# Norm sums inside the next projection's first tile, a third PSUM unit for the p-tiles, and tables made in the preceding feed-forward

## The chip, the core and the metric

The kernel is one program on one core of a Trainium2 chip. TensorE (PE in the rows) does matrix products into PSUM, VectorE (DVE) and ScalarE (ACT) do elementwise work, GpSimd (POOL) does elementwise work too, SyncE (SP) issues transfers. Each engine runs its own queue in order and waits on semaphores. The metric is the device time of one execution in microseconds, lower is better.

## What is computed

A two-layer decoder trunk for 512 prompt tokens and 8 x 8 sample tokens, so T = 576 columns, model width 1024 (8 blocks of 128 rows).

```python
def rms_norm(x, g, eps=1e-6):
    y = xf * lax.rsqrt(jnp.mean(xf * xf, axis=-1, keepdims=True) + eps)
    return (y * g.astype(jnp.float32)).astype(x.dtype)

def trunk(x, p, even_states, odd_past, W):
    for l in range(DEPTH):
        h = h + 0.5 * swiglu(rms_norm(h, W['ffn_norm1'][l]), W['ffn1_wi'][l], W['ffn1_wo'][l])
        hn = rms_norm(h, W['mix_norm'][l])
        ...
        h = h + mix
        h = h + 0.5 * swiglu(rms_norm(h, W['ffn_norm2'][l]), W['ffn2_wi'][l], W['ffn2_wo'][l])
        gate = jax.nn.sigmoid(rms_norm(h, W['ple_norm'][l]) @ W['ple_wg'][l])
        h = h + gate * (p[l] @ W['ple_wp'][l])
    return rms_norm(h, W['final_norm']), new_even, new_odd
```

The mixer of layer 0 is a 31-tap convolution beside an mLSTM, that of layer 1 is differential attention beside stick-breaking attention. There are nine norms, numbered m = 0 to 8 here as in the code: 0 and 4 before a first feed-forward, 1 and 5 before a mixer, 2 and 6 before a second feed-forward, 3 and 7 before the gated embedding (called ple), 8 at the end.

## The kernel before

Activations lie transposed: `h` is 8 blocks of [128 rows, 576 tokens]. Every product is done in a split form: an operand is rounded to a high part (`wr`, `xr`, `hr`), the rest is its low part (`wl`, `xl`, `hl`), and three matmuls (high x high, high x low, low x high: lines 399 to 401) make one product. The 576 tokens are two halves of 288, so one row block k of an output tile is 6 matmuls, and a tile of eight row blocks is 48.

**Weights** come in blocks of up to 2048 columns, in two buffers (slot 0 and slot 1). For each block SP loads `raw` (line 340), ACT rounds it to `wr` (`round_block`, line 807), POOL makes `wl` (line 389), and the semaphore `w_split0` or `w_split1` lets PE start the block. ACT rounds the block after next only when PE is done with the slot and ACT has come to it in its own queue: in each phase ACT's loop over blocks first rounds, then does the elementwise work of that block's tiles.

**A norm.** The gain is put into `xr` by ACT (`head`, line 836) and `xl` by DVE (`rest`, line 1210), without the factor 1/rms. ACT squares each block of `h` (`square`, line 826), DVE adds the squares into `acc` (lines 1219 and 1276), PE sums `acc` over partitions with a matrix of ones into PSUM banks 4 and 5 (`norm_sum`, line 441), ACT takes the root (`root`, line 841), DVE the reciprocal R (`factor`, line 1233), and R multiplies each output tile of the next projection as DVE reads it from PSUM (`normed`, line 1240). In PE's queue `norm_sum(m)` stands ahead of the projection that uses norm m.

**PSUM.** Output tiles alternate between unit 0 (banks 0, 1) and unit 1 (banks 2, 3). Unit 2 is banks 4 and 5, the norm sums and transposes; banks 6 and 7 hold convolution sums and bias rows in other stages.

**The ple phase** has 8 blocks. Block j has a gate tile (8 row blocks, 48 matmuls) and a p-tile (2 row blocks, 12 matmuls). Per block DVE scales the gate tile into `tg`, ACT takes the sigmoid `sg`, DVE multiplies the p-tile by it (`tu`) and adds to `h`, ACT squares, then ACT rounds the next weights. Ahead of it `praw` (p, transposed) is loaded, `pr` rounded by ACT (line 1055) and `pl` made by DVE (line 1581).

**Between feed-forward 2 and layer 1's attention** (norm 5) ACT issues 20 small transfers of bias tables from a scratch in memory (`strip`, `sstrip`, lines 1068 and 1075), and DVE adds masks to them (lines 1616 to 1621) and makes the scalar lambda (lines 1602 to 1612). For norms 2, 4 and 6 the `head` calls stand after the whole preceding phase, because `xr` is still being read by it.

**The start.** POOL clears both `raw` buffers (line 382) before SP may load them. ACT takes h's eight blocks in turn, and rounds the first weight block after block 4. **The end.** DVE makes R whole, then eight products with the gain, each stored by itself.

Of the kernel before, what the change touches and what calls it, by code (L numbers as in the profile page):

```python
# [16 lines left out]
F32 = mybir.dt.float32  # L17
# [101 lines left out]
def build(nc, A):  # L119
# [50 lines left out]
    brel = sb("brel", [32, HEADS * P], at=z)  # L170
    bone = sb("bone", [32, GL], at=z)
    grep = sb("grep", [P, GL], at=z)
    z = [ZONE]
    praw = sb("praw", [P, KP, T], at=z)
# [159 lines left out]
    def _(e):  # L334
# [8 lines left out]

        def load_cache(job):
# [13 lines left out]
        for name in order:  # L358
            p = ph[name]
            if name != ("out", 1):  # L360
                with e.Fori(0, p.nb // 2) as i:
                    load_pair(p, i)
                continue
# [15 lines left out]
    @block.gpsimd  # L379
    def _(e):  # L380
        for s in range(2):
            e.memset(raw[s][:], 0.0).then_inc(S(f"w_split{s}"), 1)
        for name in order:
            p = ph[name]
            with e.Fori(0, p.nb // 2) as i:
                for s in range(2):

                    e.wait_ge(S("w_rounded"), i * 2 + (p.n0 + s + 1))
                    e.tensor_tensor(wl[s][:, 0:p.width], raw[s][:, 0:p.width],  # L389
                                    wr[s][:, 0:p.width].bitcast(F32), ALU.subtract  # L390
                                    ).then_inc(S(f"w_split{s}"), 1)
# [3 lines left out]
    def _(e):  # L395
# [7 lines left out]
        def gemm(name, rhs, ready, after=None):  # L403


            p = ph[name]
            with nullcontext() if after else e.Fori(0, p.nb // 2) as loop:
                for i in range(p.nb // 2) if after else (loop,):
                    for s in range(2):
                        e.wait_ge(S(f"w_split{s}"), i + (p.n0 // 2 + 2))  # L410
                        off = 0
                        for tile, kn_ in enumerate(p.ks):
                            t = s * p.T + tile
                            u = t % 2

                            e.wait_ge(S("tile_evacuated"), i * (2 * p.T) + (p.t0 + t - 2 + 1 + CR_EVAC))
                            for k in range(kn_):
                                need = ready(tile, k) if s == 0 else None
                                if need:
                                    e.wait_ge(S(need[0]), need[1])  # L420
                                a, b = off + k * P, off + (k + 1) * P
# [1498 lines left out]
```

## Time and profile before

| | us |
|---|---|
| median of 3 runs | 2768.86 |
| lowest and highest | 2763.19, 2770.34 |
| the profiled execution, its own time | 2769.76 |
| its span, first to last instruction | 2768.0 |
| granted TensorE clock, mean | 0.945 |
| PE busy | 2614.2 |

The profile is one execution. A row of the order of time reads: start in us, duration in us, engine, line, operation, output<-input, shape, count, and in brackets the idle time before it and what ended that. Rows of matmuls overlap, as they are pipelined: the pace is the difference of their starts. A table of stretches gives each stretch's length, an engine's busy time and in brackets the number of its instructions that touch the stretch, then PEclk, the share of full clock granted (1.00 is 2.4 GHz, 0.5 is 1.2 GHz).

### The profile page before, as it was taken

How to read it: one execution, taken by the hardware profiler on the slowest of the kernel's cores; microseconds unless marked ns; L12 is line 12 of the kernel's file. 1: busy time of each engine (PE TensorE's matmuls, PEld its weight loads, DVE VectorE, ACT ScalarE, POOL GpSimd, SP SyncE). 2: the span in 40 equal slices, each digit the busy share in tenths (PEclk: the TensorE clock that was granted, in tenths of full speed). 3: DMA queues.
4: the chain of work that ended last, by engine and by line, in shares of the span. 5: the costliest groups of instructions: out<-in, count | busy, mean ns of one | idle time of the engine just before them, and what ended most of it. 6: DMA issues, size and time to landing. Idle time of an engine off the chain costs nothing. (4 is left out here: it accounts for less than half of the span.)

```text
span 2768.0 us, 44745 instructions
## 1 busy us (share of the span) xinstructions
PE 2614.2 (94%) x18322; PEld 2469.6 (89%) x18322; DVE 921.4 (33%) x1558; ACT 826.3 (30%) x998; POOL 811.5 (29%) x206
## 2 busy tenths in 40 slices
PE   6999999997889999999999999999789799999997
PEld 6999999984589999999999999999455599999997
DVE  3211224686733211223421122311755432202234
ACT  4321223223114322233432222311444433312232
POOL 3333333320022333333333333332000033333332
PEclk9999999997789999999999999999876699999999
DMA  3222223411012222222222221334311022222122
GB/s 142 78 77 100 76 69 103 84 62 45 33 63 76 79 77 88 85 66 85 91 76 83 84 90 58 112 111 152 97 61 46 16 70 82 69 98 76 68 85 72
DMA packets 66890, 220.39 MB, mean 80 GB/s; under 512 B 14006, under 2 KB 31286, under 8 KB 51194
## 3 DMA queue, kind: packets, MB, share of 16 engines
q1 hardware_dynamic: 50448, 199.49, 20.7%
q10 hardware_dynamic: 16362, 19.81, 2.5%
q8 instruction: 52, 0.85, 0.1%
q14 instruction: 28, 0.23, 0.0%
HBM read 207.95 MB, written 11.33 MB: 79 GB/s over the span
## 5 line engine op out<-in xcount | busy, mean ns | idle before, releaser
L389 POOL TENSOR_TENSOR wl<-raw,wr 128x2048 fp32r<-128x2048 f32 (+2 forms) x200 | 807.8, 4039 | 1928.7 <-ACT wr L807 1928.7
L399 PE MATMUL ps<-xr,wr 128*128 128x288 f32 x4096 | 1224.5, 299 | 8.2 <-DVE xl L1757 3.2
L400 PE MATMUL ps<-xl,wr 128*128 128x288 f32 x4096 | 1215.0, 297 | 0.0
L401 PE MATMUL ps<-xr,wl 128*128 128x288 f32 x4096 | 1210.6, 296 | 0.0
L399 PEld LDWEIGHTS ps<-xr,wr 128*128 128x128 f32 x4096 | 775.1, 189 | 12.2 <-issue 6.4
L401 PEld LDWEIGHTS ps<-xr,wl 128*128 128x128 f32 x4096 | 777.8, 190 | 0.0
L400 PEld LDWEIGHTS ps<-xl,wr 128*128 128x128 f32 x4096 | 776.1, 189 | 1.2
L807 ACT ACTIVATE wr<-raw 128x2048 fp32r<-128x2048 f32 (+1 forms) x200 | 351.7, 1759 | 373.2 <-PE ps L401 299.5
L400 PE MATMUL ps<-hl,wr 128*128 128x288 f32 x1408 | 415.3, 295 | 0.0
L401 PE MATMUL ps<-hr,wl 128*128 128x288 f32 x1408 | 415.0, 295 | 0.0
L399 PE MATMUL ps<-hr,wr 128*128 128x288 f32 x1408 | 413.2, 293 | 0.0
L399 PEld LDWEIGHTS ps<-hr,wr 128*128 128x128 f32 x1408 | 264.7, 188 | 0.9 <-DVE tu L1240 0.9
L400 PEld LDWEIGHTS ps<-hl,wr 128*128 128x128 f32 x1408 | 264.7, 188 | 0.0
L401 PEld LDWEIGHTS ps<-hr,wl 128*128 128x128 f32 x1408 | 264.5, 188 | 0.0
L1240 DVE TENSOR_TENSOR tu<-ps,R 128x576 f32<-128x576 f32 x96 | 72.8, 758 | 502.2 <-PE ps L401 502.2
L854 ACT ACTIVATE hr<-hd 128x576 f32 x88 | 60.3, 686 | 582.3 <-DVE hd L1256 582.3
L1240 DVE TENSOR_TENSOR tg<-ps,R 128x576 f32<-128x576 f32 x111 | 84.1, 758 | 328.1 <-PE ps L401 327.5
L1269 DVE SCALAR_TENSOR_TENSOR h<-ps,h 128x576 f32 x64 | 48.5, 758 | 413.1 <-PE ps L401 413.1
L851 ACT ACTIVATE sg<-tg 128x576 f32<-128x576 f32 x88 | 60.5, 687 | 205.3 <-DVE tg L1240 205.3
L836 ACT ACTIVATE xr<-h,prm 128x576 fp32r<-128x576 f32 (+1 forms) x64 | 47.3, 770 | 168.8 <-DVE h L1269 167.6
L1260 DVE TENSOR_TENSOR hl<-hd,hr 128x576 f32 x88 | 66.8, 759 | 91.4 <-ACT hr L854 91.4
L1329 DVE SCALAR_TENSOR_TENSOR ps<-up,prm,ps 128x512 f32<-128x512 f32 x116 | 87.5, 755 | 3.4 <-DVE us L1365 0.9
(305 smaller groups left out, 1690.5 us busy)
## 6 DMA issues: line engine op xcount, KB each, us to landing
raw<-in_up SPq DMA_DIRECT2D x88, 1024.0 KB, 4.8
raw<-in_down SPq DMA_DIRECT2D x32, 768.0 KB, 4.3
raw<-in_mixin SPq DMA_DIRECT2D x24, 1024.0 KB, 4.8
raw<-in_down SPq DMA_DIRECT2D x32, 640.0 KB, 3.8
raw<-in_ple SPq DMA_DIRECT2D x16, 640.0 KB, 3.8
raw<-in_mixout SPq DMA_DIRECT2D x8, 1024.0 KB, 4.9
kc<-in_kc SPq DMA_DIRECT2D x32, 256.0 KB, 3.4
vc<-in_vc SPq DMA_DIRECT2D x32, 256.0 KB, 3.4
```

The lines of the kernel that those rows point to most:

```text
L389: e.tensor_tensor(wl[s][:, 0:p.width], raw[s][:, 0:p.width], wr[s][:, 0:p.width].bitcast(F32), ALU.subtract).then_inc(S(f"w_split{s}"), 1)
L399: e.matmul(out, wrt, xrt, start=first, stop=False)
L400: e.matmul(out, wrt, xlt, start=False, stop=False)
L401: return e.matmul(out, wlt, xrt, start=False, stop=last)
L807: e.activation(wr[slot][:, 0:w], raw[slot][:, 0:w], ACT.Copy).then_inc(S("w_rounded"), 1)
L836: e.activation(xj, hj, ACT.Copy, scale=prm[:, bass.ds(j + g0, 1)]).then_inc(S("xr_ready"), 1)
L851: e.activation(sg[:], tg[:], ACT.Silu).then_inc(S("silu_ready"), 1)
L854: e.activation(hr[:, bass.ds(i * 2 + s, 1), :].rearrange("p a t -> p (a t)"), hd[:], ACT.Copy).then_inc(S("hr_ready"), 1)
L1240: ins = e.tensor_tensor(two(out), unit(u), two(R[:]), ALU.mult)
L1260: e.tensor_tensor(q, hd[:], r.bitcast(F32), ALU.subtract).then_inc(S("hidden_ready"), 1)
L1269: e.scalar_tensor_tensor(hj, unit(s), 0.5, hj, ALU.mult, ALU.add).then_inc(S("tile_evacuated"), 1)
L1329: a = e.scalar_tensor_tensor(outp, inp, w, accp, ALU.mult, ALU.add)
```

## The change

- `norm_sum(m)` for m = 0 to 7 is no longer ahead of the projection; it is emitted inside the first tile, after row block k = 6 of 8. The first pair of blocks of each projection is taken out of its loop for that. ACT's `root(m)` moves behind the first `round_block` of the phase.
- A second pair of x buffers (`xr2`, `xl2`) serves norms 2, 4 and 6, so that `head` and `rest` run inside the out and ple phases.
- In the ple phase gate tiles alternate between units 0 and 1, and p-tiles use unit 3 (banks 6, 7).
- `praw` is loaded, and `pl` made, in the preceding feed-forward's part of the queues. The bias tables are loaded by SP behind the last `down` weights, and DVE prepares them ahead of `factor(5)`; lambda follows the second tile of the attention projection. Other small tables move likewise.
- At the start the clearing of `raw` is gone, the first rounding follows h's block 0, and the first two low parts are made by POOL in four pieces each.
- At the end ACT multiplies the gain into `h` block by block in the last ple phase, DVE inverts R in halves, and four products and four stores take the place of eight.

```diff
@@ tensor
+        def unit_of(p, t):
+            return t % 2 if p.src != "ple" else 3 if t % 2 else t // 2 % 2
+        def free_before(p, t, first):
+            return 3 if p.src == "ple" and t % 2 == 0 and (t or not first) else 2
+        def gemm_pair(p, i, rhs, ready=None, after=None, norm=None):
...
+                        if norm is not None and (s, tile, k) == (0, 0, kn_ - 2):
+                            norm_sum(norm)
...
-        norm_sum(2)
         ffn(1, 2)
-        norm_sum(3)
...
@@ scalar
-        def blocks(name):
+        def blocks(name, norm=None):
             p = ph[name]
             for n in range(p.nb):
                 if not (name == order[-1] and n == p.nb - 1):
                     round_block(name, n // 2, n % 2)
+                if n == 0 and norm is not None:
+                    root(norm)
                 yield n
...
         for j in range(KD):
+            if j == 1:
+                round_block(order[0], 0, 0, first=True)
             head(0, j, (S(f"h_loaded{j}"), 16))
             square(0, j, None)
-            if j == KD // 2:
-                round_block(order[0], 0, 0, first=True)
...
         def ple(l):
             m = 4 * l + 4
-            e.dma_start(praw[:], A["pT"][l]).then_inc(S("p_loaded"), 16)
             name = ("ple", l)
-            for n in blocks(name):
-                if n == 0:
-                    e.wait_ge(S("p_loaded"), 16 * (l + 1))
-                    e.activation(pr[:], praw[:], ACT.Copy).then_inc(S("pr_ready"), 1)
+            e.wait_ge(S("p_loaded"), 16 * (l + 1))
+            e.activation(pr[:], praw[:], ACT.Copy).then_inc(S("pr_ready"), 1)
+            for n in blocks(name, 4 * l + 3):
                 e.wait_ge(S("tile_evacuated"), evac_at(name, 2 * n))
                 e.activation(sg[:], tg[:], ACT.Sigmoid).then_inc(S("ple_sig"), 1)
-                square(m, n, (S("ple_added"), KD * l + n + 1))
-            if l == 0:
-                heads_after(m)
-            root(m)
+                if l == 0:
+                    head(m, n, (S("ple_added"), KD * l + n + 1))
+                    square(m, n, None)
+                else:
+                    square(m, n, (S("ple_added"), KD * l + n + 1))
+                    e.activation(h[:, n, :], h[:, n, :], ACT.Copy, scale=W("gains", 8 * KD + n)
+                                 ).then_inc(S("h_gained"), 1)
+            if l:
+                root(m)
@@ gpsimd
         for s in range(2):
-            e.memset(raw[s][:], 0.0).then_inc(S(f"w_split{s}"), 1)
+            e.nop().then_inc(S(f"w_split{s}"), 1)
...
+        low_parts(ph[order[0]], 0, 4)
@@ vector
+            if n % 2:
+                split_p(n // 2)
+            if n == 2:
+                odd_tables()
             factor(m + 1)
...
-        for j in range(KD):
-            g = W("gains", 8 * KD + j)
-            e.scalar_tensor_tensor(h[:, j, :], h[:, j, :], g, R[:], ALU.mult, ALU.mult).then_inc(S("y_ready"), 1)
+        for hf in range(2):
+            rh = R[:, hf * HALF:(hf + 1) * HALF]
+            e.reciprocal(rh, rh).then_inc(S("R_ready"), 1)
+            e.wait_ge(S("R_ready"), 9 + hf)
+            for j in range(0, KD, 4):
+                hh = h[:, j:j + 4, hf * HALF:(hf + 1) * HALF]
+                e.tensor_tensor(hh, hh, rh.unsqueeze(1).broadcast_to([P, 4, HALF]), ALU.mult
+                                ).then_inc(S("y_ready"), 1)
```

How ACT's queue reads from the end of feed-forward 3 into the second ple phase (`wr_54` is slot 0, `wr_56` slot 1). Before:

```order
750 L841 ACTIVATE R<-ps,eps_68 128x576
751 L1050 DMA praw<-in_pT 128x1152
752 L807 ACTIVATE wr_56<-raw_53 128x1280
753 L1055 ACTIVATE pr<-praw 128x1152
754 L1057 ACT_TABLE_LOAD
755 L1057 ACTIVATE sg<-tg 128x576
756 L826 ACTIVATE sq<-h 128x576
757 L807 ACTIVATE wr_54<-raw_52 128x1280
```

And in the changed kernel:

```order
791 L1105 ACTIVATE pr<-praw 128x1152
792 L851 ACTIVATE wr_56<-raw_53 128x1280
793 L887 ACT_TABLE_LOAD
794 L887 ACTIVATE R<-ps,eps_68 128x576
795 L1108 ACT_TABLE_LOAD
796 L1108 ACTIVATE sg<-tg 128x576
797 L872 ACTIVATE sq<-h 128x576
798 L1114 ACTIVATE h<-h,prm 128x576
799 L851 ACTIVATE wr_54<-raw_52 128x1280
```

The root is now behind the rounding of slot 1, and there is one more pass over `h` between the square and the rounding of slot 0 (in the first ple phase it is the `xr` pass, `head`).

How DVE's queue reads from the end of feed-forward 2 into the attention projection. Before:

```order
753 L1276 TENSOR_TENSOR acc<-acc,sq 128x576
754 L1264 REGISTER_ALU
755 L1264 COMPARE_AND_BRANCH
756 L1233 RECIPROCAL R<-R 128x576
757 L1602 TENSOR_TENSOR lamt<-prm 128x128
```

And in the changed kernel:

```order
767 L1322 TENSOR_TENSOR acc<-acc,sq 128x576
768 L1310 REGISTER_ALU
769 L1310 COMPARE_AND_BRANCH
770 L1339 TENSOR_TENSOR strip<-strip,cst 128x128 x4
771 L1341 TENSOR_TENSOR sbias<-cst,sstrip 128x64 x4
772 L1344 MEMSET qbd 128x640
773 L1279 RECIPROCAL R<-R 128x576
```

The eight table sums and the clearing now stand between the last sum of squares and the reciprocal.

## Rows read from the trace of the kernel before

**Rows 1.** The page: busy time of each engine, its share, its instructions.
```profile
PE 2614.2 (94%) x18322; PEld 2469.6 (89%) x18322; DVE 921.4 (33%) x1558; ACT 826.3 (30%) x998; POOL 811.5 (29%) x206
```

**Rows 2.** Stretches of PE: length, busy (instructions), PEclk, DMA share, GB/s.
```profile
900.00:1200.00 300.00, 300.00 (x2257) 1.00 0.23 80
455.30:467.00 11.70, 9.29 (x44) 0.71 0.74 174
837.00:846.00 9.00, 6.64 (x35) 0.81 0.01 3
1263.40:1275.00 11.60, 7.93 (x36) 0.71 0.35 109
1334.90:1344.00 9.10, 5.88 (x30) 0.81 0.31 116
1762.00:1774.00 12.00, 8.32 (x40) 0.72 0.49 158
...
2679.40:2694.00 14.60, 10.93 (x67) 0.88 0.40 130
```

**Rows 3.** Order of time around norm 7 and the ple phase: PE, DVE, ACT, POOL.
```profile
2683.41 2.29 PE L441 MATMUL ps<-acc,ones 128*128 128x288 f32 x4 [3.67 <-DVE acc L1276]
...
2682.60 0.75 DVE L1276 TENSOR_TENSOR acc<-acc,sq 128x576 f32<-128x576 f32 x1
2686.51 3.75 DVE L1233 RECIPROCAL R<-R 128x576 f32<-128x576 f32 x1 [3.16 <-ACT R L841]
...
2692.35 0.54 DVE L1225 MEMSET acc<- 128x576 f32 x1
2692.92 0.76 DVE L1240 TENSOR_TENSOR tg<-ps,R 128x576 f32<-128x576 f32 x1
...
2680.93 0.77 ACT L836 ACTIVATE xr<-h,prm  x1 [5.42 <-DVE h L1269]
...
2689.65 1.17 ACT L1055 ACTIVATE pr<-praw 128x1152 fp32r<-128x1152 f32 x1 [2.01 <-DMA praw<-in_pT]
...
2697.94 2.94 POOL L389 TENSOR_TENSOR wl<-raw,wr 128x1280 fp32r<-128x1280 f32 x1 [7.28 <-ACT wr L807]
```

**Rows 4.** Order of time in the first ple phase: DVE, ACT, POOL.
```profile
1277.85 0.76 DVE L1240 TENSOR_TENSOR tg<-ps,R 128x576 f32<-128x576 f32 x1 [0.98 <-PE ps L401]
...
1281.62 1.90 ACT L807 ACTIVATE wr<-raw 128x2048 fp32r<-128x2048 f32 x1
...
1283.59 2.96 POOL L389 TENSOR_TENSOR wl<-raw,wr 128x1280 fp32r<-128x1280 f32 x1 [8.88 <-ACT wr L807]
```

**Rows 5.** Order of time after norm 5: DVE, POOL, PE.
```profile
1777.55 0.89 DVE L1616 TENSOR_TENSOR strip<-strip,cst 128x128 f32<-128x128 f32 x4
1778.36 0.62 DVE L1618 TENSOR_TENSOR sbias<-cst,sstrip 128x64 f32<-128x64 f32 x4
...
1778.88 4.61 POOL L389 TENSOR_TENSOR wl<-raw,wr 128x2048 fp32r<-128x2048 f32 x1 [15.45 <-ACT wr L807]
...
1783.62 0.40 PE L399 MATMUL ps<-xr,wr 128*128 128x288 f32 x1 [1.01 <-POOL wl L389]
```

**Rows 6.** Order of time at the start: POOL, DVE, PE.
```profile
16.14 4.51 POOL L389 TENSOR_TENSOR wl<-raw,wr 128x2048 fp32r<-128x2048 f32 x1 [11.84 <-ACT wr L807]
...
16.83 4.43 DVE L1210 SCALAR_TENSOR_TENSOR xl<-h,prm,xr 128x576 fp32r<-128x576 f32 x1 [1.55 <-ACT xr L836]
...
26.74 0.85 PE L399 MATMUL ps<-xr,wr 128*128 128x288 f32 x1
...
41.56 0.30 PE L399 MATMUL ps<-xr,wr 128*128 128x288 f32 x1
```

**Rows 7.** Order of time at the end: PE, DVE.
```profile
2753.38 1.24 PE L441 MATMUL ps<-acc,ones 128*128 128x288 f32 x4 [3.22 <-DVE acc L1219]
...
2755.42 3.75 DVE L1233 RECIPROCAL R<-R 128x576 f32<-128x576 f32 x1 [2.10 <-ACT R L841]
2759.21 5.92 DVE L1764 SCALAR_TENSOR_TENSOR h<-h,prm,R 128x576 f32<-128x576 f32 x8
```

More of the change, by code:

```diff
@@ L381, in _, with low_parts @@
         for s in range(2):
-            e.memset(raw[s][:], 0.0).then_inc(S(f"w_split{s}"), 1)
+            e.nop().then_inc(S(f"w_split{s}"), 1)
+        def low_parts(p, i, pieces=1):
+            for s in range(2):
+                e.wait_ge(S("w_rounded"), i * 2 + (p.n0 + s + 1))
+                n = p.width // pieces
+                for q in range(pieces):
+                    c = slice(q * n, (q + 1) * n)
+                    ins = e.tensor_tensor(wl[s][:, c], raw[s][:, c], wr[s][:, c].bitcast(F32), ALU.subtract)
+                ins.then_inc(S(f"w_split{s}"), 1)
+        low_parts(ph[order[0]], 0, 4)
         for name in order:
             p = ph[name]
[L385 to L391, printed above, removed]
+            with e.Fori(1 if name == order[0] else 0, p.nb // 2) as i:
+                low_parts(p, i)
     @block.tensor
@@ new lines, in gemm, with xin @@
+        def gemm(name, rhs, ready=None, after=None, norm=None):
+            p = ph[name]
+            gemm_pair(p, 0, rhs, ready, after, norm)
+            if after:
+                for i in range(1, p.nb // 2):
+                    gemm_pair(p, i, rhs, None, after)
+            elif p.nb > 2:
+                with e.Fori(1, p.nb // 2) as i:
+                    gemm_pair(p, i, rhs)
+        def xin(m):
+            xr_, xl_ = x_slot(m)
+            return lambda tile, k: (xr_[:, k, :], xl_[:, k, :])
@@ L779, in _ @@
         e.wait_ge(S("oc_root"), 2 * HEADS)
-        gemm(("out", 1), xin, lambda tile, k: ("mix_ready", KD + k + 1) if tile == 0 else None)
-        norm_sum(6)
+        gemm(("out", 1), xin(5), lambda tile, k: ("mix_ready", KD + k + 1) if tile == 0 else None)
         ffn(3, 6)
-        norm_sum(7)
         ple(1)
@@ L855, in up_phase @@
                                  ).then_inc(S("hr_ready"), 1)
+            if norm is not None:
+                pair(0)
+            with e.Fori(0 if norm is None else 1, p.nb // 2) as i:
+                pair(i)
         def down_phase(n, c, m_next):
@@ L1085, in _ @@
         for kind in range(2):
-            for n in blocks(f"qk{kind}"):
+            for n in blocks(f"qk{kind}", None if kind else 5):
+                if kind == 0 and n == 0:
+                    e.preload_act_table_set("natural_log_exp_and_others")
+                    e.wait_ge(S("lam_sums"), 1)
+                    e.activation(nlam[:, 0:2], nlam[:, 2:4], ACT.Exp).then_inc(S("lam_exp"), 1)
                 if kind and n < 2:
@@ L1558, in _ @@
         new_states(HEADS - 1)
-        def rests(m):
-            for j in range(KD):
-                rest(m, j)
         def out_and_norm(name, m):
```

249 lines of the change are left out of this document (132 added, 117 removed).

## Prediction

> **What bounds the kernel now.** I read the page first. PE is busy for 2614 of 2768 us, every other engine for a third or less [rows 1], so the time is PE's, and only what makes PE wait or run slowly can give anything back. Then PE's stretches. In an undisturbed one 2257 matmuls touch 300 us [rows 2], a pace of 0.133 us for each, at full clock. A norm is different: PE's last matmul before it starts, the last block of h goes through DVE, ACT and DVE, and only when the sum of squares is complete does the norm sum run (2682.60 plus 0.75, then 2683.41) [rows 3]. PE waited 3.67 us there, the granted clock fell to half, so the four norm matmuls took 2.29 us, and the next ones were slow too.
>
> What each norm costs is the length of a stretch less its matmuls at 0.133 us, two fewer than the row counts, since two only touch its edges [rows 2]. Norm 1: 11.7 - 42 x 0.133 = 6.1 us. Norm 2: 9.0 - 33 x 0.133 = 4.6, and I take norm 6, the same edge after an out phase, as 4.6 too. Norm 3: 7.1. Norm 4: 5.4. Norm 5: 6.9, and 1.0 more where PE waits for the low part of slot 1 at 1783.62, because ACT had issued 20 table transfers ahead of that rounding [rows 5]. Norm 7: 14.6 - 65 x 0.133 = 6.0. Together 41.7 us.
>
> **What the move of the norm sums gives.** With norm_sum behind row block 6, PE has 7 x 6 = 42 matmuls, 5.6 us, to do while the last block of h is made. Counted from the start of the last matmul of the old phase, the last sum of squares is complete after 3.9 us (2682.60 + 0.75, less 2679.4, the start of the norm 7 stretch) [rows 2, 3], so both the sum and the last xl are in time and the wait goes, with the clock's fall. What stays is four matmuls in the stream at full clock. They took 1.24 us at the end of the kernel [rows 7], against 0.53 for four at pace: 0.7 us. Seven times that is 4.9, so 41.7 - 4.9 = 36.8 us are to be had, if nothing else is late. The same reasoning covers norms 2, 4 and 6 only because xr2 lets head and rest run early; their cost of about 0.8 us for each block on ACT and DVE hides under tiles of 6.4 us (48 x 0.133).
>
> **What is late next: R.** It now comes from a sum that starts at 5.7 us of the new phase. From the start of a norm sum to the reciprocal are 2.04 us (2753.38 to 2755.42), the reciprocal is 3.75 [rows 7]: R is there at about 11.6. In a phase with tiles of 6.4 us the third tile, which needs the first one's PSUM unit, starts at 0.13 + 12.8 + 1.1 = 14.0 us, and the first tile is read out by 12.4. It fits with 1.6 us to spare, in norms 1, 2, 4 and 6. ACT's rounding, now ahead of the root, ends at about 4.8 (x ends at 2.3, square, then 1.9), before the root is wanted at 7, and POOL's 4.6 us end at 9.4, before 14.0.
>
> **The ple phases do not fit.** There a block is only 60 matmuls, 8.0 us. The third PSUM unit saves the PSUM wait: the second p-tile starts at 15.6 and the first is freed by 14.6. But the weights of the third block use slot 0, and ACT rounds them only after the elementwise work of the first block, which waits for R. Before, from the first tg to the end of that low part were 2697.94 + 2.94 - 2692.92 = 7.96 us in the second ple phase [rows 3] and 1283.59 + 2.96 - 1277.85 = 8.70 in the first, where the rounding is wider [rows 4]. The change puts one more ACT pass over a block of h into that chain (xr or the gain, 0.7 us beyond its overlap). R at 11.6 and the clearing of acc, 0.54 [rows 3], put tg at 12.15. The low part is ready at 12.15 + 7.96 + 0.7 = 20.8 and 21.55 us. PE wants it after two blocks and the sum, 0.13 + 120 x 0.133 + 1.1 = 17.2. That is a new wait of 3.6 and of 4.3 us. Waits of this length took the clock down in every norm above; net of the wait (3.84) and 0.7 that cost 1.5 us at norm 7 and 2.6 at norm 3, and I take 2.0. The two ple phases give back 3.6 + 4.3 + 2 x 2.0 = 11.9 us, nearly all that norms 3 and 7 gained. The split of p is not what hurts: pr takes 1.17 us [rows 3] right after the last square, and pl is made before R is wanted. In the steady part of the first ple phase the chain is 9.4 + 0.2 us from the end of a gate tile, against 1.6 + 8.0 until PE wants the weights: just enough.
>
> **The tables ahead of factor(5).** DVE's eight sums take 0.89 and 0.62 us [rows 5] and would start at 3.9, while POOL wants to start at 4.8. At the start of the kernel a DVE operation with two operands in SBUF, issued at 16.83 while POOL ran from 16.14 to 20.65, ended only at 21.26 [rows 6]: it waited for POOL's whole instruction. Two or three of the small sums would wait so, until 9.4. Then 0.6 for the rest and the clearing of qbd, R at 14.4, the first tile read at 15.2, and PE's third tile waits 1.2 us. The bounds are 0 (all eight come first) and 1.6; I take 1.2, since the order is late by half a microsecond. The transfers themselves leave ACT's queue for SP's, where they follow the last down weights; 20 issues at a third of a microsecond fill a gap that SP has between loads, and I count nothing for them, at worst 1 us. The 1.0 us wait at 1783.62 goes.
> The Trainium skill's page "SBUF — State Buffer", section "Who interferes with whom", says that a VectorE instruction with two SBUF inputs and a GpSimd instruction that reads SBUF exclude each other for a whole instruction, and that whoever issues first wins. By that rule, the trace agrees: 4.43 us for an operation over 576 columns [rows 6], where a sum over as many takes 0.75 [rows 3]. Had the two only shared bandwidth, this term would be about 0.3 by my estimate.
>
> **The start.** The first product began at 26.74 and the third tile at 41.56 [rows 6]. Now the rounding comes after block 0 of h; I estimate the weights' arrival at 7.4 us, as they no longer wait for the clearing, the rounding until 9.3, and the four pieces of the low part until 14 to 16.4, alternating with DVE. DVE still has seven blocks at about 1.5 us each and loses POOL's 4.5 us: 9.3 + 4.5 + 10.5 = 24.3, no earlier than before. But PE has done row blocks 0 to 6 by then. Norm sum at half clock 2.3 [rows 3], row block 7 at half clock 1.5, tile 1 at 6.4: the third tile starts at about 34.5 instead of 41.56, a gain of 7.0. R is in place at about 34.2. Bounds: 3, if the inputs share the transfers badly, and 10, if DVE is not held up.
>
> **The end.** R in halves costs the same 3.75, four wide products cost about as much as the 5.92 for eight [rows 7], and the last store is twice as large. I count 0.3 us lost, between a gain of 1 and a loss of 2.
>
> **The sum.** 36.8 - 11.9 - 1.2 + 7.0 - 0.3 = 30.4 us. From the profiled execution's 2769.8 that is 2739.4; the median of the runs is 0.9 lower, so I predict 2738.
>
> **Rivals.**
> 1. *The ple cover holds.* If slot 0 were rounded earlier than I read, or R came 4 us sooner, the 11.9 us stay: 2726. Against it stands the order of ACT's queue, in which the rounding of slot 0 is behind the first sigmoid. 15%.
> 2. *The start gives nothing and a further wait appears.* Input transfers compete with the weights that now load earlier, DVE ends later than 24.3, and the third tile starts about where it did; or one more place like the tables loses 3 to 5 us. 2746 to 2750. For it: DVE, not PE, sets the start, and its last sum is not earlier. 17%.
> 3. *A slow ple phase, slower than before.* The steady chain of the first ple phase has no slack (9.6 against 9.6). If it were some 2.5 us longer, PE would stop that long in every second block, and the clock would stay at half for the phase: 480 matmuls at twice 0.133, 64 us more, or 2800. It decides at stops somewhere between the 1.0 us wait at 1783.62 [rows 5], which I take as harmless, and the 3.67 us one of norm 7 [rows 3], after which the clock was at half. 3%.
> 4. *It doesn't do what it says*, the sums still end up with a wait: about no change, 2765. 2%.
> My forecast has the remaining 63%, with a range of its own of 2732 to 2745.
>
> **How the numbers follow.** The range 2724 to 2750 holds the forecast, rival 1 and rival 2; what is left out is under 2 in 10. A difference under 0.3% (8 us) could not be told from none. Faster by more than that: 0.94; within it: 0.02; slower: 0.04.
>
> **What would show it.** In the profile after, the norm sums stand among full-clock matmuls with no wait before seven of them, and PEclk stays 1.00 at norms 2, 4 and 6. In both ple phases PE waits about 4 us for POOL's wl at the third block, with the clock falling after it. After norm 5 PE waits near 1 us for DVE at the third tile. The third tile of the kernel starts near 34.5. I am wrong if the ple phases show no such wait (then nearer to 2726), if a norm's PSUM readout makes PE wait elsewhere, or if the third tile starts near 41.

## The result, and the profile after

The changed kernel takes 2721.9 us (2718.5 to 2730.0, 4 runs) against 2768.1 before: the ratio is 0.9838, 95% interval 0.9816 to 0.9861. That is 46 us less, where 30 were forecast, and 2 us below the low end of the range. The profiled executions differ by 49.6 us. The page of after, first lines, answers to [rows 1]:

```profile
span 2718.4 us, 44463 instructions
PE 2574.8 (95%) x18322; PEld 2441.8 (90%) x18322; DVE 921.6 (34%) x1555; ACT 772.8 (28%) x962; POOL 811.0 (30%) x210
```

PE makes the same 18322 matmuls and is busy 39 us less with them. Waits that go away don't shorten busy time; a higher clock and a quicker pace do. That line alone says that much of the gain is of a kind that the forecast didn't have.

Stretches of PE at norms 1, 2, 3 (with the third ple block), 5 and 7, and the third block of the second ple phase, of after (length, busy (instructions) of PE, PEld, DVE, ACT and POOL, granted clock, DMA share, GB/s). They answer to [rows 2]:

```profile
447.00:458.70 11.70, 11.70 (x80) 10.72 (x79) 4.78 (x7) 6.57 (x6) 5.96 (x2) 1.00 0.41 131
826.50:835.50 9.00, 9.00 (x67) 8.79 (x66) 4.78 (x3) 3.09 (x4) 3.75 (x1) 1.00 0.35 118
1256.00:1275.00 19.00, 14.65 (x92) 14.42 (x91) 9.19 (x11) 6.92 (x8) 5.81 (x2) 0.82 0.21 70
1730.00:1742.00 12.00, 10.86 (x82) 10.63 (x81) 5.60 (x14) 6.57 (x6) 6.44 (x2) 1.00 0.31 120
2630.00:2645.00 15.00, 15.00 (x110) 14.59 (x108) 10.60 (x10) 8.78 (x11) 2.93 (x1) 1.00 0.16 53
2640.00:2660.00 20.00, 16.35 (x105) 16.12 (x105) 8.81 (x10) 6.97 (x9) 5.81 (x2) 0.83 0.19 66
```

A norm is now 11.7 of 11.7 us busy at full clock, where it was 9.29 at 0.71; norms 2 and 7 likewise. The idle time has moved. These are PE's waits for weights, in the order of time of after: the start of the kernel, the third block of the first ple phase, the first block of the phase behind norm 4, the first block behind norm 5, the third block of the second ple phase.

```profile
17.35 0.58 PE L434 MATMUL ps<-xr,wr 128*128 128x288 f32 x1 [17.35 <-POOL wl L419]
1262.67 0.60 PE L434 MATMUL ps<-xr,wr 128*128 128x288 f32 x1 [4.35 <-POOL wl L419]
1315.59 0.41 PE L434 MATMUL ps<-xr,wr 128*128 128x288 f32 x1 [1.65 <-POOL wl L419]
1736.85 0.40 PE L434 MATMUL ps<-xr,wr 128*128 128x288 f32 x1 [1.14 <-POOL wl L419]
2648.70 0.60 PE L434 MATMUL ps<-xr,wr 128*128 128x288 f32 x1 [3.65 <-POOL wl L419]
```

The two long ones are the ple waits that the forecast named, at 4.3 and 3.6 us. The matmul behind each takes 0.60 in place of 0.40: the clock had fallen to half. Behind the 1.65 and the 1.14 us it had not.

I then laid the two traces side by side by matmul number, and took the gain of each stage (all from the profiled executions, in us):

| Stage | forecast | measured |
|---|---|---|
| start, up to the end of the first feed-forward | 7.0 | 6.3 |
| norm 1 and the projections behind it | 5.4 | 3.9 |
| mLSTM (its own matmuls) | 0 | **6.0** |
| norm 2 | 3.9 | 3.9 |
| norms 3 and 4, first ple phase | 4.8 | 1.9 |
| norm 5 and the projections behind it | 6.0 | 6.4 |
| attention (its own matmuls) | 0 | **11.3** |
| norm 6 | 3.9 | 5.0 |
| norm 7, second ple phase | -0.3 | -0.6 |
| pace of the matmuls that read xr2 and xl2 | 0 | **7.0** |
| end | -0.3 | -1.4 |
| sum | 30.4 | 49.6 |

What the forecast had terms for gave 25.4 us in place of 30.4 (the rows are rounded, and their sum is off by 0.1). The miss is in the three bold rows, 24.2 us, for which it had none. Both mixers have the same instructions in either kernel. Their whole length in before and after, mLSTM and then attention (columns as above):

```profile
643.10:783.80 140.70, 105.32 (x338) 68.59 (x336) 85.09 (x186) 34.13 (x67) 0.68 (x1) 0.68 0.10 36
1927.70:2199.40 271.70, 226.87 (x1096) 132.40 (x1094) 148.32 (x388) 115.05 (x276) 0.00 (x0) 0.73 0.19 60
```
```profile
632.90:767.60 134.70, 99.59 (x337) 63.08 (x336) 84.89 (x186) 34.12 (x67) 0.62 (x1) 0.72 0.11 37
1894.70:2155.20 260.50, 208.26 (x1096) 122.84 (x1094) 148.00 (x388) 115.14 (x276) 0.00 (x0) 0.80 0.19 62
```

VectorE and ScalarE do the same amount of work in the same time (148.3 and 148.0, 115.1 and 115.1). PE has the same matmuls, but its mean granted clock is 0.80 in place of 0.73. Summed over the clock's records, the attention spent 144.5 us at half clock before and 102.0 after, the mLSTM 90.9 and 76.4.

### The profile page after: what moved, and what is told of

Same layout as the page of the kernel before. It is cut to its first block, busy times and chain, and to the rows that moved or that the text cites. A ratio compares the mean times of both kernels' runs of the same rounds, so it can differ in the third digit from the quotient of the medians.

```text
span 2718.4 us, 44463 instructions
## 1 busy us (share of the span) xinstructions
PE 2574.8 (95%) x18322; PEld 2441.8 (90%) x18322; DVE 921.6 (34%) x1555; ACT 772.8 (28%) x962; POOL 811.0 (30%) x210
## 4 chain that ended last, share of the span: by engine, by line
issue 78%; POOL 14%; PE 6%; POOLq 0%; DVE 0%; DMA 0%; ACT 0%; DVEq 0%; SPq 0%; ACTq 0%
POOL wl L419 14%; PE ps L434 2%; PE ps L435 2%; PE ps L436 2%; POOLq L425 0%; DMA raw<-in_up 0%; DVE h L1833 0%; ACT wr L851 0%; DVE R L1829 0%; PE ps L494 0%; POOLq L415 0%; PE ps L550 0%; DVEq L1971 0%; DVE acc L1265 0%; DVE h L1671 0%
## 5 line engine op out<-in xcount | busy, mean ns | idle before, releaser
L419 POOL TENSOR_TENSOR wl<-raw,wr 128x2048 fp32r<-128x2048 f32 (+3 forms) x206 | 810.7, 3937 | 1879.2 <-ACT wr L851 1879.2
L903 ACT ACTIVATE hr<-hd 128x576 f32 (+1 forms) x88 | 60.3, 686 | 564.7 <-DVE hd L1302 564.7
L882 ACT ACTIVATE xr<-h,prm 128x576 fp32r<-128x576 f32 (+1 forms) x64 | 49.6, 776 | 252.5 <-DVE h L1315 167.2
```

Of the source, the lines that this page charges most:

```text
L419: ins = e.tensor_tensor(wl[s][:, c], raw[s][:, c], wr[s][:, c].bitcast(F32), ALU.subtract)
L882: e.activation(xj, hj, ACT.Copy, scale=prm[:, bass.ds(j + g0, 1)]).then_inc(S("xr_ready"), 1)
L903: e.activation(hr[:, bass.ds(i * 2 + s, 1), :].rearrange("p a t -> p (a t)"), hd[:], ACT.Copy).then_inc(S("hr_ready"), 1)
```

## The experiments

Eighteen more runs were made, two of them of the two kernels as they are. Where a run has one execution only, its verdict rests on its trace, by stages, and not on its total.

### Is it the same again?

The kernel before and the changed kernel, as they are.

> The kernel before once more, for a second profile. Theory A (the windows in which the clock is set run free of the kernel, and where their edges fall decides how much of the mixers runs at half clock): the offset of the clock's steps from the kernel's start differs from the first profile's, and the mLSTM and attention stretches differ from 140.7 and 271.7 us by several us, with more or less time at half clock. Rival B (the change itself shortens the mixers): 140.7 and about 271 again, whatever the offset.

> The changed kernel once more, for a second profile. Theory A (the mixers' part of the gain is the granted clock, which falls differently in each execution): the stretch from the first score matmul after norm 5's projections to the first product of the second out phase, 260 us in the profile of the change and 272 in that of before, comes out different by several us with the same instructions, and so does the mLSTM stretch (134 against 140). Rival B (something in the change itself shortens the mixers): 260 and 134 again within 1 us. Ratio to before 0.982 to 0.985 either way.

Before: 2769.6 in one execution, mLSTM 140.7, attention 271.7, the waits where they were. After: 2720.8 (2718.3 to 2733.0, 4 runs), ratio 0.986 [0.9816, 0.9903]; mLSTM 134.8, attention 260.2. So the bold rows stand in two profiles of each kernel.

### The pace of the matmuls

In undisturbed stretches the matmuls that read xr and xl follow each other in 133.3 ns, those that read xr2 and xl2 (new in the changed kernel) or hr and hl in 132.2. The same 140 us of the second feed-forward's first up-projection, in before (with xr) and in after (with xr2):

```profile
860.00:1000.00 140.00, 140.00 (x1053) 140.00 (x1052) 33.36 (x44) 47.90 (x43) 49.42 (x11) 1.00 0.22 77
```
```profile
841.00:981.00 140.00, 140.00 (x1061) 140.00 (x1060) 33.35 (x44) 34.55 (x33) 50.51 (x12) 1.00 0.22 77
```

Eight matmuls more in the same time. 6336 matmuls moved to xr2: 6336 x 1.1 ns = 7.0 us. By the program's layout, in bytes along a partition, xr, xl and all weight buffers begin whole multiples of 128 apart, and xr2, xl2, hr and hl 64 past such a place. Two rivals: the matmul is slow because of where its moving tile begins by itself, or because moving tile and weights are alike modulo 128. The edits put 64 unused bytes ahead of xr (which moves all that lies behind it, the weights too), and in two of the kernels 64 more ahead of raw, so that the weights are back in their old place modulo 128 and xr is not:

```
+    sb("pad0", [P, 16])
     XR_AT = top[0]
     xr = sb("xr", [P, KD, T], F32R)
     xl = sb("xl", [P, KD, T], F32R)
+    sb("pad1", [P, 16])
     raw = [sb(f"raw{s}", [P, BLK]) for s in range(2)]
```

> The change with one gap of 64 bytes, ahead of xr alone, so that the weights and everything behind move by 64 too. Theory A1 (the place of the moving tile alone counts): xr matmuls at 132.22 ns, hr and xr2 matmuls now at 133.33. Theory A2 (the place of the moving tile relative to the weights counts: slow when both are alike modulo 128): xr matmuls stay at 133.33, hr and xr2 matmuls stay at 132.22. Rival B (no placement effect): paces as in the change.

> The change with 64 bytes left free ahead of xr and 64 ahead of raw, so that xr and xl begin 64 bytes off a multiple of 128, as xr2, xl2, hr and hl do, and the weights stay on a multiple of 128. Theory A (a matmul is 1.1 ns slower when its moving tile begins on a multiple of 128 bytes): the up-projection of the first feed-forward goes from 133.33 to 132.22 ns a matmul, some 6000 matmuls gain, 6 to 7 us less than the change. Rival B (the faster pace belongs to something else about the second pair, such as who wrote it last): 133.33 ns stays, no difference.

> The kernel before with the same two gaps of 64 bytes and nothing else. Theory A (placement): all 12288 matmuls that read xr or xl go from 133.33 to 132.22 ns, 13.6 us less, ratio to before 0.995. Rival B: ratio 1.000. A third case, that the pace is hidden by other engines somewhere, would give a ratio between.

The same 140 us of the first up-projection, in the kernel with the first gap alone and in the one with both; only PE's count is of interest:

```profile
50.00:190.00 140.00, 140.00 (x1046) 139.23 (x1046) 33.02 (x44) 36.13 (x34) 49.33 (x12) 1.00 0.22 77
```
```profile
50.00:190.00 140.00, 140.00 (x1054) 139.23 (x1053) 33.02 (x44) 36.00 (x34) 50.55 (x12) 1.00 0.22 78
```

With one gap xr begins 64 further on, where xr2 was modulo 128, and is as slow as before (133.33 ns from 50 to 170 us): its weights moved with it. With both, 1054 in the same time, 132.22 ns. So it is the relation of the two; distances other than 0 and 64 were not tried. The kernel with the first gap alone took 2715.7 in its one execution. The changed kernel with both gaps takes 2713.1 us (2711.6 to 2721.3, 4 runs), ratio 0.9827 [0.9787, 0.9867]; the kernel before with both 2746.6 (2734.1 to 2751.1, 9 runs), ratio 0.9915 [0.9892, 0.9939]. That is more than the pace gives the latter (14 us for 0.995): in the profiled one 7.6 us are the attention's, which took 264.1. The Trainium skill's page "SBUF — State Buffer", section "Who interferes with whom", lists TensorE's read of the moving tile and its weight load as independent ports; these counts show that where the two lie still costs 0.8% of a matmul.

### The norm sums put back

All eight sums that the change moved stand ahead of the projection again; the rest of the change stays.

```
             p = ph[name]
-            gemm_pair(p, 0, rhs, ready, after, norm)
+            if norm is not None:
+                norm_sum(norm)
+            gemm_pair(p, 0, rhs, ready, after)
```

> The change with each norm sum again ahead of its projection (norms 0 to 7), all else kept: second x pair, p-tiles in unit 3, tables, start, end. Theory A (the prediction's working): seven waits of 2.5 to 3.9 us with their half clock come back, 36.8 us less the two late weight waits in the ple phases, which the earlier wait hides again (about 9 of 12 us), and less the 1 to 2 us waits at norms 4 and 5: 24 to 28 us more than the change, about 2747; at the start 2 to 5 us of it. Rival B (most of the gain came from the other parts): under 12 us more.

2754.6 us (2743.9 to 2770.2, 10 runs), ratio 0.9967 [0.9938, 0.9995]: 34 us of the 46 hang on the place of the sums, with all that it brings in the mixers. The waits are back (3.24 at norm 2, 3.67 and 4.65 at norms 3 and 4, where before had 2.36, 3.67 and 3.22), the ple waits are gone, the first product starts at 27.2 and the third tile at 42.2, and both mixers are back too: 140.6 and 272.7. The profiled execution was the longest of the ten, so the others need not have had mixers as long. That asked which of the norms does that to the mixers. Two kernels split them: norms 1 and 5, the last ahead of mLSTM and attention, put back alone, and norms 2, 3, 4, 6 and 7 (norm 0's sum stays inside the tile in both). The edit of the first:

```
-                        if norm is not None and (s, tile, k) == (0, 0, kn_ - 2):
+                        if norm not in (None, 1, 5) and (s, tile, k) == (0, 0, kn_ - 2):
                             norm_sum(norm)
...
+            if norm in (1, 5):
+                norm_sum(norm)
             gemm_pair(p, 0, rhs, ready, after, norm)
```

> The changed kernel with the norm sums 1 and 5 alone put back ahead of the projection that follows them; these are the last norms ahead of the mLSTM and of the attention. By their rows that gives back 5.3 + 6.4 = 11.7 us. Theory 'the idle stretch of a norm and the half clock behind it shape the mixer that follows': mLSTM back from 134.8 to 140.7 us and attention from 260.3 to 271.7 us, so 11.7 + 17 = 29 us slower than the changed kernel, about 2750. Rival 'the mixers' gain has another cause (the general load of the kernel, or which moment of the clock the mixer happens to meet)': mixers at 134 to 135 and 258 to 261 us, about 2733.

> The complement: the norm sums 2, 3, 4, 6 and 7 put back, 1 and 5 left inside the next projection's first tile. By their rows these give back 22 to 24 us less about 9 us of the waits in the per-layer phases, which disappear. Theory 'norms 1 and 5 shape the mixers': mLSTM stays at 134.8 and attention at 260.3 us, about 2735. Rival 'the general load does': both mixers partly or wholly back to 140.7 and 271.7 us, 2740 to 2752.

The first takes 2732.7 (2728.3 to 2733.9, 4 runs), ratio 0.9881 [0.986, 0.9902], the second 2740.0 (2726.1 to 2747.8, 4 runs), 0.9902 [0.9867, 0.9936]. mLSTM and attention of the first, then of the second:

```profile
637.00:777.60 140.60, 105.28 (x338) 68.51 (x336) 85.03 (x186) 34.12 (x67) 0.68 (x1) 0.68 0.10 36
1908.10:2167.80 259.70, 206.32 (x1096) 122.25 (x1094) 147.84 (x388) 115.17 (x276) 0.00 (x0) 0.82 0.19 62
```
```profile
631.70:769.50 137.80, 101.67 (x338) 65.97 (x336) 85.03 (x186) 34.12 (x67) 0.67 (x1) 0.71 0.11 36
1907.50:2176.60 269.10, 225.76 (x1096) 131.30 (x1093) 148.09 (x388) 114.98 (x276) 0.00 (x0) 0.74 0.19 60
```

Half of my theory held. With norm 1's idle stretch the mLSTM takes 140.6 to 140.7 in all five profiles that have it with nothing added behind it (the kernel before in two executions and with the gaps, all sums back, and sums 1 and 5 back); without it, 133.9 to 138.0 in eight. But norm 5 doesn't hold the attention: it is short with norm 5 back and long with norm 5 in place. The theory that one idle stretch shapes the mixer behind it fell for the attention.

### The moment at which a mixer begins

What is left is when a mixer begins, since the changes of the clock may then fall on other instructions. In the kernel before I added products to the last tile ahead of each mixer, in five amounts (0.5, 1.1, 1.6, 2.4 and 2.9 us), ahead of the tile's first real product, which clears the bank. In all five the loop of the projection ahead of the mLSTM is written out as well, so that its last tile can be told apart:

```
                                 r, q = rhs(tile, k)
+                                if (name, t, k) == ("v1", 3, 0) or ((name, t, k) == ("qo", 3, 0) and i == 1):
+                                    for _ in range(12):
+                                        e.matmul(ps[:, 2 * u, 0:HALF], wr[s][:, a:b], r[:, 0:HALF], start=True, stop=True)
```

> The kernel before with twelve products (some 1.6 us at the full clock) made twice in the last tile of the projection ahead of the mLSTM, and twelve in the last tile ahead of the attention; the first of the real products clears the bank, so the output stays. Both mixers start some 1.6 us later against whatever sets the clock's steps, and nothing else changes. Theory 'the moment at which a mixer meets the clock's steps decides its time at half clock': the mLSTM falls from 140.7 to 134 or 135 us, and the attention moves too, so that the kernel is faster by 3 to 15 us in spite of 3.2 us of added work. Rival 'the moment is of no account': 140.7 and 271.7 us and 3.2 us slower, 2772.

> The kernel before with 4 added products (0.5 us) in the last tile ahead of each mixer. Theory 'a mixer has a few courses, and the moment it begins decides between them': over the five shifts tried the mLSTM takes anything from 134 to 141 us and the attention 258 or 272 us, and at least one of the five reaches the short times. Rival 'the course hangs on what the change does elsewhere': every shift leaves 139 to 141 and 264 to 272 us.

> The same with 8 added products (1.1 us) at each of the two places. Theory and rival as for the run with 4 products; 1.6 us gave 139.2 and 270.1.

> The same with 18 added products (2.4 us) at each of the two places. Theory and rival as for the run with 4 products.

> The same with 22 added products (2.9 us) at each of the two places. Theory and rival as for the run with 4 products.

| added products | 0 | 4 | 8 | 12 | 18 | 22 |
|---|---|---|---|---|---|---|
| attention, us | 271.7 | 271.2 | 258.8 | 270.1 | 264.4 | 260.4 |
| at half clock | 144.5 | 144.5 | 95.2 | 141.1 | 122.5 | 98.6 |
| mLSTM, us | 140.7 | 140.2 | 139.9 | 139.2 | 136.9 | 137.9 |
| start of the attention, us | 1927.7 | 1925.5 | 1928.9 | 1928.4 | 1928.6 | 1928.5 |
| this execution, us | 2769.8 | 2766.8 | 2759.1 | 2768.8 | 2764.0 | 2759.9 |

The attention with 8 added products, in the kernel before:

```profile
1928.90:2187.70 258.80, 205.46 (x1096) 121.49 (x1094) 147.95 (x388) 115.08 (x275) 0.00 (x0) 0.82 0.19 63
```

So in the kernel before the attention can be as short as in the changed one (258.8 against 260.5). That the added amount does it is not shown. Each column is one execution, and counted from the kernel's first instruction the attention did not begin in the order of the amounts: with 4 products it began 2.2 us earlier than with none. The kernel with 12 products took 2768.4 in the median (2764.3 to 2769.7, 10 runs), ratio 1.0006 [0.9995, 1.0017]. And the kernel before with nothing added scatters as far: of the 42 executions of it that ran beside these experiments, five took 2747.0 to 2758.4 at a mean granted clock of 0.950 to 0.958, where the median is 2768.2 at 0.945. The course can come from the execution. Courses fork at a point that can be seen: some 82 us in, the clock falls to half for 3.4 us in before and for 10.2 us in after, and then the rest runs with less half clock in after. First the spell in before and one of those that follow it, then the spell in after and the stretch behind it:

```profile
2010.50:2013.90 3.40, 3.30 (x8) 0.64 (x8) 2.42 (x8) 1.02 (x4) 0.00 (x0) 0.50 0.00 0
2027.60:2037.80 10.20, 10.15 (x29) 4.08 (x27) 5.99 (x15) 3.98 (x8) 0.00 (x0) 0.50 0.01 2
```
```profile
1978.10:1988.30 10.20, 10.20 (x39) 4.69 (x36) 3.35 (x14) 2.05 (x7) 0.00 (x0) 0.50 0.33 108
1988.30:1998.60 10.30, 9.40 (x75) 7.11 (x71) 6.26 (x20) 6.55 (x16) 0.00 (x0) 1.00 0.31 98
```

In all twenty profiles a longer spell at that place goes with less half clock behind it: those with 258 to 261 us have the long one, and 264 to 273 us come with the short one.

The mLSTM fell only by what was added (140.7 less 0.5, 1.1, 1.6, 2.9 us), or 1.4 us more at 18 products. Counted from norm 1's sum, its end stayed within 1.3 us in all six. Some 9 us in, PE waits for VectorE, for 5.91 us in before and 4.32 with 12 products: that wait took up the added time. VectorE's part is fed from the first projection on, and was not moved. So twelve and twenty products went into the first tile of that projection (glu), right behind norm 1; its loop is written out too:

```
+                                if (name, t, k, i) == ("glu", 0, 0, 0):
+                                    for _ in range(12):
```

> The kernel before with 12 added products (1.6 us) in the first tile behind norm 1, ahead of the projections that feed the mLSTM; nothing else. Theory 'norm 1's idle stretch sets the moment at which the mLSTM's whole chain, VectorE's part too, meets the clock's steps': the mLSTM takes 134 to 138 us in place of 140.7. Rival 'the mLSTM's time hangs on something else': 140.6 to 140.7 us again, as in all five kernels that kept norm 1's idle stretch.

> The same with 20 added products (2.6 us). Theory: 134 to 138 us. Rival: 140.6 to 140.7 us.

```profile
652.30:786.30 134.00, 98.47 (x339) 61.86 (x337) 84.83 (x186) 34.12 (x67) 0.65 (x1) 0.73 0.11 37
```
```profile
642.60:784.50 141.90, 108.62 (x339) 69.83 (x337) 84.91 (x186) 34.12 (x67) 0.63 (x1) 0.66 0.10 35
```

With 12 the mLSTM takes 134.0, with 20 it takes 141.9, in one execution each (2769.5 and 2770.5 in all). So norm 1's idle stretch doesn't by itself hold the mLSTM at 140.6. But the 12 products moved more than their 1.6 us. Two of VectorE's small operations now met POOL's low parts and took 4.95 and 4.53 us, where they take 0.50 and 0.20 in before. The rows show the second, which in before ended ahead of POOL's start. PE waits 8.12 us for `kT`, and 1.53 in before. Before first, then the kernel with 12:

```profile
532.40 0.20 DVE L1406 TENSOR_TENSOR rows<-prm,rows 4x64 f32<-4x64 f32 x1
```
```profile
534.51 4.49 POOL L389 TENSOR_TENSOR wl<-raw,wr 128x2048 fp32r<-128x2048 f32 x1 [8.13 <-ACT wr L810]
534.56 4.53 DVE L1409 TENSOR_TENSOR rows<-prm,rows 4x64 f32<-4x64 f32 x1
540.55 0.58 PE L399 MATMUL ps<-xr,wr 128*128 128x288 f32 x1 [8.12 <-DVE kT L1245]
```

The mLSTM began 9.2 us later than in before, and what it saved was spent ahead of it. With the wait goes a spell at half clock. The same 10.2 us of it and of before:

```profile
535.90:546.10 10.20, 5.55 (x23) 5.58 (x24) 5.14 (x5) 0.94 (x2) 3.11 (x1) 0.50 0.30 104
```
```profile
535.90:546.10 10.20, 10.20 (x80) 10.20 (x79) 5.24 (x11) 0.75 (x2) 3.34 (x1) 1.00 0.29 104
```

### The ple phases

ACT rounds the weights of block n + 1 ahead of the elementwise work of block n, and the first of them ahead of the root:

```
-            for n in blocks(name, 4 * l + 3):
+            rounding(0)
+            root(4 * l + 3)
+            for n in range(KD):
+                rounding(n + 1)
                 e.wait_ge(S("tile_evacuated"), evac_at(name, 2 * n))
```

> The change with ACT's queue in the ple phases turned by one step: the rounding for the block after next stands ahead of the sigmoid of this block, not behind its square. Theory A (the wait of 4.6 and 4.0 us at the third block, and the one of 2.0 before the next up-projection, are slot 0 being rounded too late): all three gone, with the clock's fall behind them, 12 to 14 us less than the change, about 2708. Rival B (POOL or the reading of PSUM is what is late): the waits shrink by under 2 us each, nothing measurable in all.

2717.1 us (2706.8 to 2720.6, 4 runs), ratio 0.9842 [0.9793, 0.9891]. The stretches of both third blocks, which were 14.65 of 19 and 16.35 of 20 us busy:

```profile
2640.00:2660.00 20.00, 20.00 (x152) 20.00 (x152) 11.88 (x10) 7.32 (x11) 8.88 (x3) 1.00 0.20 67
1256.00:1275.00 19.00, 19.00 (x145) 19.00 (x144) 12.62 (x14) 8.50 (x11) 6.64 (x3) 1.00 0.25 79
```

The cause named in the forecast, ACT's order, was right: both waits are gone, and the two ple stages are 5.5 and 6.2 us shorter. A wait of 2.5 us remains ahead of the next feed-forward, and the first matmul behind it takes 0.58: the clock was at half. Here the earlier low part runs into VectorE's last sum for h (POOL, DVE and PE of the same kernel in order of time; start, duration):

```profile
1301.70 4.62 POOL L419 TENSOR_TENSOR wl<-raw,wr 128x2048 fp32r<-128x2048 f32 x1 [5.67 <-ACT wr L851]
1302.23 0.76 DVE L1676 TENSOR_TENSOR tu<-ps,sg 128x576 f32<-128x576 f32 x1 [2.52 <-ACT sg L1115]
1303.02 3.91 DVE L1678 TENSOR_TENSOR h<-h,tu 128x576 f32<-128x576 f32 x1
...
1310.09 0.58 PE L434 MATMUL ps<-xr,wr 128*128 128x288 f32 x1 [2.50 <-issue]
```

The sum of two SBUF operands takes 3.91 us while POOL runs, the one with ps as an operand 0.76 in the same time. The median gained only 3.7 us on the changed kernel, and not 11.7. The profiled execution took 2706.8 at a mean granted clock of 0.962, although its mLSTM was 3.1 us longer than in after; the other three took 2714.7 to 2720.6 at 0.951 to 0.954. They have no trace, and how much of this is the mixers' can't be told.

### The start

The change's own edits to the start taken back (the clearing of raw, the rounding after half of the blocks, the low part in one piece), norm 0's sum left inside the tile.

> The change with the old start: raw cleared by POOL, first rounding behind block 4 of h, low parts in one piece. The norm sum stays inside the first tile. Theory A (the start's gain is the earlier first product, which runs under DVE's work on h): first product at about 22 us instead of 17.35, third tile 3 to 5 us later than 35.21. Rival B (the gain is the norm sum's move alone, since DVE ends at 24.95 or 25.4 either way): third tile within 1.5 us of 35.21.

2721.1 in one run. The first product starts at 21.3 (17.4 in after, 26.7 before) and the third tile at 37.4 (35.2 in after, 41.6 before) [rows 6]: with the sum inside the tile these edits are worth 2.2 us, and its place the other 4.1. By themselves they give nothing: with the sums put back and these edits kept, the third tile started at 42.2.

### A faster version

The changed kernel with both gaps, the early rounding in the ple phases, the old end, and in each feed-forward's last down phase ScalarE's rounding for the next block ahead of the copy and square of h:

```
+            if c == 1:
+                round_block(("down", n, c), 0, 0)
+                for j in range(KD):
+                    if j + 1 < KD:
+                        round_block(("down", n, c), (j + 1) // 2, (j + 1) % 2)
+                    head(m_next, j, (S("tile_evacuated"), evac_at(("down", n, c), j)))
+                    square(m_next, j, None)
+                return
```

> The changed kernel with four edits: 64 bytes of gap ahead of xr and 64 ahead of the weight buffers (measured alone: 2713.1), the per-layer phases' weight rounding one block early (measured alone: 3.7 us of median gain), ScalarE's rounding of the weight block ahead of the normalised strip's copy and square in the last down phase of each feed-forward, which should end the wait of 1.43 us at norm 5, and the end of the kernel as before (-1.4 us). Theory that they add up: 2713 - 3.7 - 1.4 - 1.4 = 2706 to 2707. Rival 'they overlap': 2709 to 2713, since the early rounding costs waits elsewhere (DVE and POOL hold each other up) and the mixers keep their own scatter.

**2701.2 us** (2697.9 to 2715.4, 5 runs), ratio 0.9778 [0.9751, 0.9806], the fastest of all. Norm 5 has no wait left; the stretch is 13.0 of 13.0 us busy:

```profile
1727.00:1740.00 13.00, 13.00 (x97) 12.79 (x97) 9.91 (x15) 6.47 (x6) 6.16 (x2) 1.00 0.29 87
```

That is below its own forecast of 2706, which lies within its scatter, although its profiled execution met a long mLSTM (138.0) and a long attention (267.0); that one took 2710.9, three of the other four 2697.9 to 2701.2.

## Why the prediction was right and wrong

**The norms.** Right. PE's waits ahead of the sums are gone and the clock stays up. Norm 1 with its projections gave 3.9 of 5.4 us. The norm itself gave 5.2; the rest was lost in the projections, where a spell at half clock lasted 13.7 us (from 568.3 us) in place of 10.2. Norm 2 gave 3.9 of 3.9 and norm 6 5.0 of 3.9, but taking norm 6 to cost what norm 2 costs was right: across each of the two the distance between the traces grows by the same 4.3 us. The other 0.8 of norm 6's row fall in the first products behind the attention, which its last spell at half clock still covers.

**The ple phases.** Right in place, cause and size: 3.65 and 4.35 us where 3.6 and 4.3 stood, with half clock behind them. Wait and half clock together cost 6.2 and 7.0 us where 5.6 and 6.3 stood. The early rounding showed the cause. What the step left out is what is next in the queue: 1.65 us at 1315.59, where POOL's low part for the first block behind norm 4 ends too late. Before, norm 4's own wait hid it; with the sums put back it is gone again. Norm 4 gave 3.1 where 4.7 stood, and the stage 1.9 of 4.8.

**Norm 5.** The size was right (6.4 of 6.0) by luck, and the mechanism wrong. I had VectorE's table sums wait for POOL, and PE's third tile for them. The rows of after, DVE and POOL:

```profile
1739.25 0.89 DVE L1339 TENSOR_TENSOR strip<-strip,cst 128x128 f32<-128x128 f32 x4
1740.06 0.63 DVE L1341 TENSOR_TENSOR sbias<-cst,sstrip 128x64 f32<-128x64 f32 x4
```
```profile
1732.20 4.59 POOL L419 TENSOR_TENSOR wl<-raw,wr 128x2048 fp32r<-128x2048 f32 x1 [5.62 <-ACT wr L851]
1740.15 4.99 POOL L419 TENSOR_TENSOR wl<-raw,wr 128x2048 fp32r<-128x2048 f32 x1 [3.35 <-ACT wr L851]
```

The sums had nearly ended when POOL came, and it was POOL that took 0.4 us longer; nobody waited. The 1.14 us that PE does wait are for the low part of 1732.20, whose rounding stands in ACT's queue behind the copy and square of the last block but one. The forecast asked of R what is late next, and not of the first weights of the phase behind a norm. The reordered down phase took this wait away.

**The start.** Right: third tile at 35.2 where 34.5 stood, 6.3 of 7.0 us.

**The end.** Mis-sized: -1.4 where -0.3 stood, and for other reasons. PE and DVE of after, to be held against [rows 7]:

```profile
2702.39 2.29 PE L494 MATMUL ps<-acc,ones 128*128 128x288 f32 x4 [3.22 <-DVE acc L1265]
...
2705.49 1.95 DVE L1829 RECIPROCAL R<-R 128x288 f32<-128x288 f32 x1 [3.15 <-ACT R L887]
2707.47 2.63 DVE L1833 TENSOR_TENSOR h<-h,R 128x1152 f32<-128x1152 f32 x2
...
2710.02 1.95 DVE L1829 RECIPROCAL R<-R 128x288 f32<-128x288 f32 x1
2712.00 2.63 DVE L1833 TENSOR_TENSOR h<-h,R 128x1152 f32<-128x1152 f32 x2
```

From the first reciprocal to the last product are 9.1 us (2705.49 to 2714.63) where 9.7 were (2755.42 to 2765.13): 0.6 gained. The last norm sum took 2.29 in place of 1.24, with its clock at half, so R began 1.1 later. From the last product to the end of the span are 3.8 us in place of 2.9, since the last store is twice as large: 0.9. The faster version, with the old end, has 2.8 there again.

**The step that failed** is the first one: "only what makes PE wait or run slowly can give anything back", and then only the norms were looked at. Two things make PE slow that the sum had no term for. The 0.133 us of a matmul was taken as a constant [rows 2], and where the operands lie moved it (7.0 us). And the clock was followed only behind the norms, while 235 of the 303 us that before spent at half clock lie in the two mixers; in the changed kernel these run another course (17.2 us less in this profile; of the eight executions of the changed kernel two took 2730.0 and 2733.0, 9 to 15 us above five of the others). Neither could have been priced closely ahead, but a range that takes in some 10 us for stretches with a mixed clock would have held the time. No rival named it. Rival 1's 2726 is nearer to the measured time than the forecast, but by luck: it had the ple waits gone, and both are there.

**What stays open.** What sets a mixer's course is not shown. The same instructions run long and short in either kernel and with or without added work; the shifts have one execution each but one, and don't separate the amount added from the execution. Medians and profiles say only that the changed kernel met the short attention more often than the kernel before. Nor is it shown why norm 1's idle stretch goes with 140.6 us of mLSTM in the five profiles that have it with nothing added.

## What to carry to other kernels

When a change removes a wait at a place where several queues meet, ask of each of them, the weights' path included, what arrives last then; the old wait was hiding it. Before you take a matmul's pace as fixed, compare its pace between buffers, and look at where moving tile and weights begin modulo 128 bytes: here two gaps of 64 bytes gave 6.5 us by the pace of the matmuls that still read xr, and 7.7 in the median. Where a stretch runs at a mixed clock, its length belongs to the execution more than to the edit: compare several executions, and credit an edit by its own stage.

## What the runs showed of the hardware

- A matmul of 288 columns follows the last in 133.3 ns where the moving tile and the weights begin alike modulo 128 bytes, and in 132.2 where they lie 64 apart; the start of the moving tile by itself makes no difference.
- The attention ran on courses of 258.5 to 272.7 us in twenty profiles with the same instructions in it, with 92 to 148 us of it at half clock. Four added products ahead of it gave 271.2 and eight 258.8, in one execution each.
- Behind waits of 1.14 and 1.65 us in a dense stretch the clock stayed up. Behind 2.36 (norm 2 in before) and 2.50 (early rounding) it was at half for 3.4 us, behind 3.65 and 4.35 for 6.8 (3.4 behind one of 4.35, with the first gap alone).
- A VectorE sum of two SBUF operands took 3.91 us beside a POOL operation of 4.62, where it takes 0.76 alone; a sum of 4 x 64 elements took 4.53 beside one of 4.49, and 0.20 alone. Where the small sums were first, POOL took 4.99 in place of 4.59.
